# Fourteen quads of weight blocks by Strassen's seven products in a two-layer attention encoder

## The chip, the cores and the metric

The kernel runs on one core of one Trainium2 chip, as one launch. What counts is the device time of that core in microseconds. Below, TensorE is called PE, VectorE DVE, ScalarE ACT, SyncE SP and GpSimd POOL.

## The reference

x is 256 tokens by 4096 features, float32. There are two layers. In the first, h = rms_norm(x) is multiplied by w_in_ab (4096 x 13312) into queries, keys and values of two groups of attention heads (A: 16 query heads, 4 key heads, rotary positions; B: 16 heads in a neighbourhood with a bias) and a gate; y = attention x silu(gate), and x = x + y @ w_out_ab (4096 x 4096). The second is the same in form: w_in_c (4096 x 10240), 32 query heads and 8 key heads in a window with a sink, then x = x + y @ w_out_c. A last rms_norm is applied.

```
for layer in range(2):
    h = rms_norm(x, norm_w[layer])
    z = h @ w_in[layer]                       # q, k, v, gate
    y = attention(q, k, v) * silu(gate)       # (256, 4096)
    x = x + y @ w_out[layer]                  # (4096, 4096)
return rms_norm(x, final_norm_w)
```

## The kernel before, in words

Nearly all of the work is four matrix products of a 256 x 4096 activation with weights that are read once. Each operand is float32 and is cut into two parts of type fp32r, `hi` (rounded) and `lo` (the rest); a product takes three matmuls, hi x hi, hi x lo and lo x hi (`three_passes`, L1096, the matmuls on L1098, L1099 and L1100).

**Pairs and blocks.** `plan` (L155) cuts the columns into 31 pairs of two groups g = 0, 1 of 512 columns. A pair has NB = 32 blocks; a block (g, c) is the 256 rows 2c and 2c+1 (in chunks of 128) of one group, so 128 x 1024 elements in SBUF. `Pair.blocks` gives their order: `BLOCKS` (14 of group 0, 14 of group 1, then the last two of each) or `IN_TURN` (all 16 of group 0, then all of group 1). For a block PE does 2 row chunks x 2 token tiles x 3 passes = 12 matmuls of 512 columns into the two PSUM banks `proj[g][0]` and `proj[g][1]` (`product`, L1124). I number the pairs from 0; pair 6 is the first of `vg` columns, pairs 7 to 12 are a loop of three rounds of two pairs, 13 to 16 write x1 (14 to 16 a loop of three rounds), 17 to 26 are the second layer's input products, 27 to 30 write x2. The other loops hold one pair.

**How a block flows.** Every engine walks the same list of steps b = 0..31 of each pair, in program order. SP loads block b into ring slot b % 4 of `raw` once `w_lo` of block b-4 is made (`body`, L497). At step b, ACT makes `w_hi` of block b+2 when PE has done block b-2 (`split_hi_at`, L629, the activation on L637), then DVE makes `w_lo` of it (`split_lo`, L751, the subtraction on L757), and PE waits for `lo_ready`. When a group's last block is done, its two banks are drained: by ACT and, for v, DVE (`drain` L640, `drain_v` L785), or by DVE alone with the residual (`add_x1` L979, `add_x2` L1000). With `BLOCKS` group 0 is drained at step 30, with `IN_TURN` at step 16; group 1 at step 0 of the next pair.

**What else runs.** A pair with side A, B or C also holds the attention of four heads. One with side `qk`, `h` or `k` turns tiles: DVE transposes them at steps 0 and 3, they go through DRAM, and ACT and DVE split them at the third and fourth numbers of `BOTH_TURNS` or `K_TURN` (steps 5 and 9). The pairs with side "none" have only the drain. In the changed kernel no pair with attention has a quad.

The lines around the change:

```
if b == p.done0 and p.out == "x1":        # DVE, step b, after split_lo
    add_x1(0, p.n)
with eng.Fori(0, rounds) as i:            # a loop of the plan, on every engine
    for p in pairs:
        body(p.at(i))
```

## Time and profile before

| | us |
|---|---|
| median of 3 runs (lowest, highest) | 2814.05 (2813.85, 2814.28) |
| profiled execution, its own time | 2814.37 |
| its span, first to last instruction | 2812.6 |
| PE matmul busy | 2797.6 (99%), 12681 matmuls |
| DVE busy | 1687.7 (60%) |
| ACT busy | 1347.7 (48%) |
| DMA engines, mean share | 0.68 on the main queue, 226 GB/s of HBM |
| granted PE clock, mean | 0.998 |

The span leaves out 1.8 us that lie around the instructions. Matmuls overlap in the records: one is shown for 0.39 us though the next starts after 0.23 us, so the pace is read from start to start and not from the durations.

### The profile page before, as it was taken

What the parts mean: (1) busy time and instruction counts of PE and PEld (TensorE: products, weight loads), DVE (VectorE), ACT (ScalarE), POOL (GpSimd) and SP (SyncE); (2) the same over time, 40 slices, a digit from 0 to 9 for tenths busy, and PEclk for the clock granted to TensorE, in tenths of its full rate; (3) what the DMA queues carried; (4) which work ended last, traced back from release to release, by engine and by line L of the source; (5) the groups of instructions that cost most, each with busy time, mean ns of one, the idle gap of its engine ahead of it and who ended that gap; (6) DMA issues with size and microseconds to landing.
All of it is one profiled execution on the core that took longest, in us unless ns stands there. A gap on an engine that the chain in (4) does not pass through costs nothing.

```text
span 2812.6 us, 37759 instructions
## 1 busy us (share of the span) xinstructions
PE 2797.6 (99%) x12681; PEld 2329.4 (83%) x12681; DVE 1687.7 (60%) x2103; ACT 1347.7 (48%) x1654; POOL 16.4 (1%) x14
## 2 busy tenths in 40 slices
PE   9999999999999999999999999999999999999998
PEld 7888888888888888888888888888888888888886
DVE  7766666556556555566665556666655666665554
ACT  6455455445444444444443445555544455543333
POOL 0000000000000000000000000000000000000000
PEclk9999999999999999999999999999999999999999
DMA  9777777777767777677777767777676777676665
GB/s 334 222 210 232 225 226 221 224 217 228 234 209 215 228 220 239 189 254 254 253 240 222 223 211 218 231 233 220 221 226 204 231 227 225 216 251 218 215 209 187
DMA packets 357923, 637.17 MB, mean 227 GB/s; under 512 B 25376, under 2 KB 79136, under 8 KB 357792
## 3 DMA queue, kind: packets, MB, share of 16 engines
q1 hardware_dynamic: 343824, 593.52, 67.7%
q10 hardware_dynamic: 13968, 41.95, 4.1%
q8 instruction: 76, 1.25, 0.2%
q14 instruction: 55, 0.45, 0.1%
HBM read 585.56 MB, written 49.81 MB: 226 GB/s over the span
## 4 chain that ended last, share of the span: by engine, by line
PE 99%; DMA 0%; issue 0%; DVE 0%; ACT 0%; POOLq 0%; POOL 0%; SPq 0%; DVEq 0%; ACTq 0%
PE proj L1098 32%; PE proj L1099 32%; PE proj L1100 32%; PE o_ps L1099 1%; PE o_ps L1098 1%; PE sc_ps L1100 1%; PE o_ps L1100 1%; PE sc_ps L1099 1%; PE sc_ps L1098 1%; DMA raw<-in_w_in_ab 0%; DVE w_lo L757 0%; DVE x_fin L1091 0%; ACT w_hi L637 0%; POOLq L268 0%; POOL rms L598 0%
## 5 line engine op out<-in xcount | busy, mean ns | idle before, releaser
L757 DVE TENSOR_TENSOR w_lo<-raw,w_hi 128x1024 fp32r<-128x1024 f32 x990 | 1208.5, 1221 | 856.7 <-ACT w_hi L637 850.5
L637 ACT ACTIVATE w_hi<-raw 128x1024 fp32r<-128x1024 f32 x990 | 1049.6, 1060 | 1148.6 <-PE proj L1100 1087.3
L1098 PE MATMUL proj<-w_hi,h_hi 128*128 128x512 f32 x2936 | 1143.4, 389 | 2.0 <-issue 1.5
L1099 PE MATMUL proj<-w_lo,h_hi 128*128 128x512 f32 x2936 | 1142.8, 389 | 0.0
L1100 PE MATMUL proj<-w_hi,h_lo 128*128 128x512 f32 x2936 | 1142.1, 389 | 0.0
L1100 PEld LDWEIGHTS proj<-w_hi,h_lo 128*128 128x128 f32 x2936 | 551.2, 188 | 114.9
L1098 PEld LDWEIGHTS proj<-w_hi,h_hi 128*128 128x128 f32 x2936 | 551.4, 188 | 114.5 <-issue 2.4
L1099 PEld LDWEIGHTS proj<-w_lo,h_hi 128*128 128x128 f32 x2936 | 551.4, 188 | 109.9
L1098 PE MATMUL proj<-w_hi,y_hi 128*128 128x512 f32 x1024 | 398.4, 389 | 0.0
L1099 PE MATMUL proj<-w_lo,y_hi 128*128 128x512 f32 x1024 | 398.4, 389 | 0.0
L1100 PE MATMUL proj<-w_hi,y_lo 128*128 128x512 f32 x1024 | 398.3, 389 | 0.0
L1100 PEld LDWEIGHTS proj<-w_hi,y_lo 128*128 128x128 f32 x1024 | 192.2, 188 | 39.9
L1099 PEld LDWEIGHTS proj<-w_lo,y_hi 128*128 128x128 f32 x1024 | 192.3, 188 | 39.3
L1098 PEld LDWEIGHTS proj<-w_hi,y_hi 128*128 128x128 f32 x1024 | 192.3, 188 | 39.3
L912 DVE TENSOR_TENSOR y<-o_ps,head_land 128x256 f32<-128x256 f32 x64 | 27.2, 425 | 109.3 <-PE o_ps L1100 109.3
L736 ACT ACTIVATE y_hi<-y 128x256 f32 (+1 forms) x64 | 26.8, 419 | 94.9 <-DVE y L912 94.9
L704 ACT ACTIVATE probs<-sc_ps,exp_bias 128x256 f32<-128x256 f32 x96 | 44.7, 470 | 46.8 <-DVE exp_bias L899 34.7
L728 ACT ACTIVATE headT_hi<-head_land 128x512 fp32r<-128x512 f32 x64 | 40.5, 633 | 54.0 <-DMA head_land<-head_turn 51.6
L905 DVE TENSOR_TENSOR headT_lo<-head_land,headT_hi 128x512 fp32r<-128x512 f32 x64 | 43.9, 686 | 10.1 <-ACT headT_hi L728 9.8
L924 DVE STREAM_TRANSPOSE head_stage<-probs 128x512 f32<-128x512 f32 x64 | 44.3, 692 | 0.0
L887 DVE SCALAR_TENSOR_TENSOR sc_ps<-dist,slope,sc_ps 128x512 f32<-128x512 f32 x32 | 24.2, 756 | 28.9 <-PE sc_ps L1100 27.3
L891 DVE TENSOR_REDUCE neg_max<-sc_ps 128x2 f32<-128x512 f32 x48 | 33.2, 691 | 11.5 <-PE sc_ps L1100 9.6
(115 smaller groups left out, 975.5 us busy)
## 6 DMA issues: line engine op xcount, KB each, us to landing
raw<-in_w_in_ab SPq DMA_DIRECT2D x414, 512.0 KB, 4.4
raw<-in_w_in_c SPq DMA_DIRECT2D x320, 512.0 KB, 4.4
raw<-in_w_out_ab SPq DMA_DIRECT2D x128, 512.0 KB, 4.5
raw<-in_w_out_c SPq DMA_DIRECT2D x128, 512.0 KB, 4.5
head_turn<-head_stage SPq DMA_DIRECT2D x256, 96.0 KB, 1.9
head_land<-head_turn ACTq DMA_DIRECT2D x64, 384.0 KB, 5.5
landing<-group_turn ACTq DMA_DIRECT2D x31, 512.0 KB, 5.5
group_turn<-q_stage SPq DMA_DIRECT2D x64, 128.0 KB, 3.2
```

Source lines behind the costliest of these rows:

```text
L637: nc.scalar.activation(w_hi[:, slot], raw[:, slot], ACT.Copy).then_inc(hi_ready, 1)
L704: last = nc.scalar.activation(probs[:, t], sc_ps[:, t], ACT.Exp, bias=exp_bias[:, t:t + 1], scale=scale, accum_out=sums[:, t:t + 1])
L728: nc.scalar.activation(headT_hi[:, :, :2 * TT], head_land[:, :, :2 * TT], ACT.Copy) \
L736: nc.scalar.activation(y_hi[:, bass.ds(row, 1)].rearrange("p a n -> p (a n)"), y[:], ACT.Copy) \
L757: nc.vector.tensor_tensor(w_lo[:, slot], raw[:, slot], w_hi[:, slot].bitcast(F32), ALU.subtract) \
L891: nc.vector.tensor_reduce(dst[:], sc_ps[:], AX_X, ALU.max, negate=True).then_inc(maxima, 1)
L905: nc.vector.tensor_tensor(headT_lo[:, :, :2 * TT], head_land[:, :, :2 * TT], headT_hi[:, :, :2 * TT].bitcast(F32), ALU.subtract) \
L912: nc.vector.tensor_tensor(y[:].rearrange("p (t q r) -> p t q r", t=TT, q=NQ), o_ps[:].rearrange("p (t q r) -> p t q r", t=TT, q=NQ), gateT ...
L924: nc.vector.transpose(columns[:, :2 * TT], probs[:].rearrange("p t (k j r) -> p (t k) j r", k=TT, j=NQ))
L1098: nc.tensor.matmul(dst, hi, r_hi, start=start, stop=False)
L1099: nc.tensor.matmul(dst, hi, r_lo, start=False, stop=False)
L1100: return nc.tensor.matmul(dst, lo, r_hi, start=False, stop=stop)
```

## The change

Fourteen times four blocks, (0, c1), (1, c1), (1, c2), (0, c2), are taken together as a quad: a 2 x 2 arrangement of weight blocks B11, B12, B22, B21 and of activation tiles (two token tiles by two row pairs). Eight products of 6 matmuls become seven (the form of Winograd): four of the left factors are sums of activation tiles, made once for several pairs (`make_sums`, at the steps in `combine`), and the right factors are four blocks and three mixes of blocks, made by DVE in each quad. PE's product r reads slot (start + r/2) % 4 of `w_hi` and `w_lo` if r is even, else one of two spare slots (`weights_of`). SP, ACT, DVE and PE each keep four steps for a quad. PE's steps hold products 0 and 1, 2 and 3, 4 and 5, and 6. The products go to the banks x11, x12, x21, x22 (the old `proj`) and to three more, m1, m6, m7 (m7 shares the bank of `o_ps`).

After the last quad of a pair ACT copies m1 to SBUF and DVE folds m1, m6 and m7 into the four banks in seven additions (`fold`); the fifth completes x12. Group 1 starts after that, on the folded banks, at block `second_at`. I write q for the first block of a pair's last quad. Quads stand in pairs 6, 8 and 10 (`VG_QUADS`, q = 12, `second_at` = 18 = q+6), 14, 15, 16 and 28 (`X1_QUADS`, the same numbers), 18, 23 and 29 (`TWO_QUADS`, quads at 5 and 13, `second_at` = 20 = q+7) and 30 (`LAST_QUADS`, quad at 9, `second_at` = 16 = q+7). In these pairs group 0 is done and drained before group 1 begins, at step 18, 20 or 16. The counters `lo_ready`, `hi_ready` and `block_done` now count products, a quad for 8. The loop of two pairs has two rounds in place of three, its last two pairs stand alone, and so do the pairs of the loops of x1 and of x2. `K_TURN` splits at step 9 and not 5.

```diff
+def with_quads(first, second, end=()):
+    blocks, quads = [], {}
+    for e in first:
+        if isinstance(e, tuple):
+            c1, c2 = e
+            quads[len(blocks)] = e
+            blocks += [(0, c1), (1, c1), (1, c2), (0, c2)]
+        else:
+            blocks.append((0, e))
+    return blocks + [(1, c) for c in second] + list(end), quads
...
+REST1, REST2 = [0, 1, *range(4, KC // 2)], [0, 1, *range(6, KC // 2)]
+VG_QUADS = with_quads([*REST1[:12], (2, 3), *REST1[12:]], REST1)
+X1_QUADS = with_quads([*REST1[:12], (2, 3), *REST1[12:]], REST1)
+TWO_QUADS = with_quads([*REST2[:5], (2, 3), *REST2[5:9], (4, 5), *REST2[9:]], REST2)
+LAST_QUADS = with_quads([*REST1[:9], (2, 3), *REST1[9:-2]], REST1[:-2],
+                        [(g, EARLY + c) for g in range(2) for c in range(LATE)])
...
-K_NORM_TURN, K_TURN = (0, 5, 7, 10), (0, 0, 2, 5)
+K_NORM_TURN, K_TURN = (0, 5, 7, 10), (0, 0, 2, 9)
...
-        (1, [Pair("in_ab", vg(0), "vg", "qk", "qk", v=1)]),
-        (3, [Pair("in_ab", qk(1), "qk", "B", "vg", batch=4), Pair("in_ab", vg(1), "vg", "qk", "qk", v=2)]),
+        (1, [Pair("in_ab", vg(0), "vg", "qk", "qk", v=1, quads=VG_QUADS, heads=16, combine=((5, "vg", 0, 2),))]),
+        (2, [Pair("in_ab", qk(1), "qk", "B", "vg", batch=4),
+             Pair("in_ab", vg(1), "vg", "qk", "qk", v=2, quads=VG_QUADS, heads=20, heads_step=4)]),
+        (1, [Pair("in_ab", qk(3), "qk", "B", "vg", batch=6)]),
+        (1, [Pair("in_ab", vg(3), "vg", "qk", "qk", v=4)]),
         (1, [Pair("out_ab", out_cols(0), "x1", "B", "vg", batch=7)]),
-        (3, [Pair("out_ab", out_cols(1), "x1", "h", "x1", x_batch=0)]),
-        (1, [Pair("in_c", kvc(0), "kv", "h", "x1", x_batch=3)]),
-        (1, [Pair("in_c", c(0), "qg", "k", "kv", v=5)]),
+        (1, [Pair("out_ab", out_cols(1), "x1", "h", "x1", x_batch=0, quads=X1_QUADS, heads=32,
+                  combine=((6, "x1", 0, 2),))]),
+        (1, [Pair("out_ab", out_cols(2), "x1", "h", "x1", x_batch=1, quads=X1_QUADS, heads=32)]),
+        (1, [Pair("out_ab", out_cols(3), "x1", "h", "x1", x_batch=2, quads=X1_QUADS, heads=32, spare="x1_end")]),
+        (1, [Pair("in_c", kvc(0), "kv", "h", "x1", x_batch=3, combine=((15, "qg", 0, 2), (19, "qg", 1, 4)))]),
+        (1, [Pair("in_c", c(0), "qg", "k", "kv", v=5, quads=TWO_QUADS, heads=32)]),
         (3, [Pair("in_c", c(1), "qg", "C", "qg", batch=8)]),
         (1, [Pair("in_c", kvc(1), "kv", "C", "qg", batch=11)]),
-        (1, [Pair("in_c", c(4), "qg", "k", "kv", v=6)]),
+        (1, [Pair("in_c", c(4), "qg", "k", "kv", v=6, quads=TWO_QUADS, heads=48)]),
         (3, [Pair("in_c", c(5), "qg", "C", "qg", batch=12)]),
         (1, [Pair("out_c", out_cols(0), "x2", "C", "qg", batch=15)]),
-        (2, [Pair("out_c", out_cols(1), "x2", "none", "x2")]),
-        (1, [Pair("out_c", out_cols(3), "x2", "none", "x2")]),
+        (1, [Pair("out_c", out_cols(1), "x2", "none", "x2", quads=X1_QUADS, heads=64,
+                  combine=((6, "x2", 0, 2), (26, "x2", 1, 4)))]),
+        (1, [Pair("out_c", out_cols(2), "x2", "none", "x2", quads=TWO_QUADS, heads=64)]),
+        (1, [Pair("out_c", out_cols(3), "x2", "none", "x2", quads=LAST_QUADS, heads=64)]),
...
+def slot_free_after(p, m):
+    if m >= NB + RING:
+        return p.o + p.op[NB] + m - NB - RING + 1
+    return p.o + (p.ring_op[m - RING] if m >= RING else m - RING) + 1
...
+        def weights_of(p, start, r):
+            if r % 2 == 0:
+                slot = (start + r // 2) % RING
+                return w_hi[:, slot], w_lo[:, slot]
+            return [tile[:] for tile in spare_of[p.spare][r // 2 % 2]]
...
                 for b, (g, c) in enumerate(p.blocks):
-                    if isinstance(p.n, int) and p.n * NB + b < RING:
-                        pass
-                    else:
-                        sp.wait_ge(lo_ready, p.n * NB + b - RING + 1)
+                    if b >= RING and p.quad_at(b - RING) is not None and p.quad_at(b - RING)[2] < 3:
+                        k, _, part = p.quad_at(b - RING)
+                        sp.wait_ge(mixed, QUAD * (p.quad_n + k) + part + 1)
+                    elif b >= RING:
+                        sp.wait_ge(lo_ready, p.o + p.freed[b - RING])
+                    elif p.n0 > 0:
...
+            def quad_hi(p, k, start, part):
+                n = p.o + p.op[start]
+                (mix, mix3), mixes_done = mix_of[p.out], QUAD * (p.quad_n + k)
+                b11, _, b22, b21 = (raw[:, (start + r) % RING] for r in range(QUAD))
+                earlier = p.o + p.op[list(p.quads)[k - 1]] if k > 0 else None
+                def hi(r, source, count=1):
+                    if r % 2 == 0:
+                        act.wait_ge(block_done, slot_free_after(p, start + r // 2))
+                    elif r == 5:
+                        act.wait_ge(block_done, n + 2)
+                    elif earlier is not None:
+                        act.wait_ge(block_done, earlier + (6 if r == 1 else 4))
+                    elif r == 1:
+                        act.wait_ge(block_done, p.o)
+                        act.wait_ge(folded, p.folds)
+                        act.wait_ge(sums_split, p.combined + (1 if p.combine else 0))
+                    dst, _ = weights_of(p, start, r)
+                    nc.scalar.activation(dst, source, ACT.Copy).then_inc(hi_ready, count)
+                if part == 0:
+                    raw_landed(p, start)
+                    hi(0, b11)
+                if part == 1:
+                    raw_landed(p, start + 2)
+                    hi(1, b22)
+                if part == 2:
+                    act.wait_ge(mixed, mixes_done + 1)
+                    hi(2, mix[:])
+                    act.wait_ge(mixed, mixes_done + 2)
+                    hi(3, mix3[:])
+                if part == 3:
+                    raw_landed(p, start + 3)
+                    hi(4, b21)
+                    act.wait_ge(mixed, mixes_done + 3)
+                    hi(5, mix[:])
+                    act.wait_ge(mixed, mixes_done + 4)
+                    hi(6, b21, 2)
...
+            def copy_m1(p, b):
+                if p.quads and b == p.last_quad + QUAD:
+                    act.wait_ge(folded, p.folds)
+                    act.wait_ge(block_done, p.o + p.op[p.last_quad] + OPS)
+                    nc.scalar.activation(folds_of(p)[0], m1[:], ACT.Copy).then_inc(m1_copied, 1)
...
+            def quad_lo(p, k, start, part):
+                n = p.o + p.op[start]
+                mix, mix3 = (tile[:] for tile in mix_of[p.out])
+                mixes_done = QUAD * (p.quad_n + k)
+                b11, b12, b22, b21 = (raw[:, (start + r) % RING] for r in range(QUAD))
+                minus = lambda dst, a, b: nc.vector.tensor_tensor(dst, a, b, ALU.subtract)
+                def lo(r, source, count=1):
+                    hi, dst = weights_of(p, start, r)
+                    dve.wait_ge(hi_ready, n + r + 1)
+                    minus(dst, source, hi.bitcast(F32)).then_inc(lo_ready, count)
+                if part == 0:
+                    lo(0, b11)
+                if part == 1:
+                    second = (start + 1) % RING
+                    dve.wait_ge(raw_loaded[second], 16 * (p.n * (NB // RING) + (start + 1) // RING + (second > 1)))
+                    dve.wait_ge(lo_ready, n + 1)
+                    minus(mix, b12, b11).then_inc(mixed, 1)
+                    lo(1, b22)
+                if part == 2:
+                    dve.wait_ge(mixed, mixes_done + 1)
+                    minus(mix3, b22, b12).then_inc(mixed, 1)
+                    lo(2, mix)
+                    dve.wait_ge(mixed, mixes_done + 2)
+                    dve.wait_ge(lo_ready, n + 3)
+                    minus(mix, b22, mix).then_inc(mixed, 1)
+                    lo(3, mix3)
+                if part == 3:
+                    lo(4, b21)
+                    dve.wait_ge(mixed, mixes_done + 3)
+                    dve.wait_ge(lo_ready, n + 5)
+                    minus(b21, b21, mix).then_inc(mixed, 1)
+                    lo(5, mix)
+                    dve.wait_ge(mixed, mixes_done + 4)
+                    lo(6, b21, 2)
+                    dve.wait_ge(lo_ready, n + OPS)
...
+            def make_sums(p, b):
+                for k, (at, stage, quad, c1) in enumerate(p.combine):
+                    if b not in (at, at + 1):
+                        continue
...
+                    rows = slice(2 * c1, 2 * c1 + 4)
+                    a_hi, a_lo = (y_hi, y_lo) if p.w in ("out_ab", "out_c") else (h_hi, h_lo)
+                    dve.wait_ge(block_done, p.o)
+                    if p.out == "vg":
+                        dve.wait_ge(turned, p.x0 + 2)
+                    dve.wait_ge(sums_split, p.combined + k)
+                    nc.vector.tensor_tensor(parts, a_hi[:, rows].bitcast(F32), a_lo[:, rows].bitcast(F32), ALU.add) \
+                        .then_inc(sums_made, 1)
+                    a11, a12 = parts[:, 0:2, 0:P], parts[:, 2:4, 0:P]
+                    a21, a22 = parts[:, 0:2, P:SEQ], parts[:, 2:4, P:SEQ]
+                    s1, s2, s3, s4 = (sums[:, r] for r in range(4))
+                    dve.wait_ge(sums_made, done + 1)
+                    nc.vector.tensor_tensor(s3, a11, a21, ALU.subtract)
+                    nc.vector.tensor_tensor(s1, a21, a22, ALU.add).then_inc(sums_made, 1)
+                    dve.wait_ge(sums_made, done + 2)
+                    nc.vector.tensor_tensor(s2, s1, a11, ALU.subtract).then_inc(sums_made, 1)
+                    dve.wait_ge(sums_made, done + 3)
+                    nc.vector.tensor_tensor(s4, a12, s2, ALU.subtract).then_inc(sums_made, 1)
...
+            def fold(p, b):
+                add = lambda dst, a, b: nc.vector.tensor_tensor(dst, a, b, ALU.add).then_inc(folded, 1)
+                (x11, x21), (x12, x22) = [[bank[:] for bank in group] for group in proj]
+                f1, f2, f3 = folds_of(p)
+                if b == p.last_quad + QUAD:
+                    dve.wait_ge(m1_copied, p.pair_w + 1)
+                    dve.wait_ge(block_done, p.o + p.op[p.last_quad] + OPS)
+                    add(f2, m6[:], f1)
+                    dve.wait_ge(folded, p.folds + 1)
+                    add(f3, m7[:], f2)
+                if b == p.last_quad + QUAD + 1:
+                    dve.wait_ge(folded, p.folds + 2)
+                    add(f2, x22, f2)
+                    dve.wait_ge(folded, p.folds + 3)
+                    add(x22, x22, f3)
+                    add(x12, x12, f2)
+                if b == p.second_at:
+                    dve.wait_ge(block_done, p.o + p.op[p.second_at])
+                    add(x11, x11, f1)
+                    add(x21, x21, f3)
+                    dve.wait_ge(folded, p.folds + FOLDS)
...
+                if p.quads and b == p.second_at:
+                    pe.wait_ge(folded, p.folds + 5)
...
+            def quad(p, k, start, part):
...
+                def times(r, left, dst, first, final, count=1):
+                    right_hi, right_lo = weights_of(p, start, r)
+                    pe.wait_ge(lo_ready, n + r + 1)
+                    for j, (a_hi, a_lo) in enumerate(left):
+                        last = three_passes(dst[:], a_hi, a_lo, right_hi[:, j], right_lo[:, j],
+                                            first and j == 0, final and j == 1)
+                    last.then_inc(block_done, count)
+                if part == 0:
+                    if opens:
+                        pe.wait_ge(drained[1], 2 * p.n)
+                        pe.wait_ge(y_made, p.heads)
+                        pe.wait_ge(sums_split, p.combined + (1 if p.combine else 0))
+                    times(0, of_tile(c1, 0), m1, opens, closes)
+                    times(1, of_sum(3), x12, opens, closes)
+                if part == 1:
+                    times(2, of_sum(0), x22, opens, closes)
+                    times(3, of_sum(2), m7, opens, closes)
+                if part == 2:
+                    times(4, of_tile(c2, 0), x11, False, False)
+                    times(5, of_sum(1), m6, opens, closes)
+                if part == 3:
+                    times(6, of_tile(c2, 1), x21, False, False, 2)
...
```

## Rows read from the trace of the kernel before

**Rows 1.** The page: busy time of each engine, chain that ended last.
```profile
PE 2797.6 (99%) x12681; PEld 2329.4 (83%) x12681; DVE 1687.7 (60%) x2103; ACT 1347.7 (48%) x1654; POOL 16.4 (1%) x14
```

**Rows 2.** Waits of PE: line, releaser: us in total, times, longest.
```profile
PE proj L1098 <- issue: 1.5, 2, 0.8
PE proj L1098 <- DVE w_lo L757: 0.5, 1, 0.5
```

**Rows 3.** Timeline (start, us, instruction), PE, first matmuls of pairs 14 and 15.
```profile
1274.63 0.39 PE L1098 MATMUL proj<-w_hi,y_hi 128*128 128x512 f32 x1
...
1361.45 0.39 PE L1100 MATMUL proj<-w_hi,y_lo 128*128 128x512 f32 x1
1361.67 0.39 PE L1098 MATMUL proj<-w_hi,y_hi 128*128 128x512 f32 x1
```

**Rows 4.** Timeline, PE, at a back edge of the two-pair loop.
```profile
1000.50 0.39 PE L1100 MATMUL proj<-w_hi,h_lo 128*128 128x512 f32 x1
1001.64 0.49 PE L1098 MATMUL proj<-w_hi,h_hi 128*128 128x512 f32 x1 [0.76 <-issue]
1001.97 0.39 PE L1099 MATMUL proj<-w_lo,h_hi 128*128 128x512 f32 x1
```

**Rows 5.** Timeline of one block in pair 6: PE starts it; ACT; DVE.
```profile
588.10 0.39 PE L1098 MATMUL proj<-w_hi,h_hi 128*128 128x512 f32 x1
...
588.35 1.06 ACT L637 ACTIVATE w_hi<-raw 128x1024 fp32r<-128x1024 f32 x1 [1.66 <-PE proj L1100]
...
589.51 1.23 DVE L757 TENSOR_TENSOR w_lo<-raw,w_hi 128x1024 fp32r<-128x1024 f32 x1 [1.49 <-ACT w_hi L637]
```

**Rows 6.** Lines: instructions, count, busy us, mean ns, idle before.
```profile
L757 DVE TENSOR_TENSOR w_lo<-raw,w_hi 128x1024 fp32r<-128x1024 f32 x990 | 1208.5, 1221 | 856.7 <-ACT w_hi L637 850.5 <-DVE w_lo L757 1.0
...
L637 ACT ACTIVATE w_hi<-raw 128x1024 fp32r<-128x1024 f32 x990 | 1049.6, 1060 | 1148.6 <-PE proj L1100 1087.3 <-DMA raw<-in_w_in_ab 18.5 <-DMA head_turn<-head_stage 13.0
...
L887 DVE SCALAR_TENSOR_TENSOR sc_ps<-dist,slope,sc_ps 128x512 f32<-128x512 f32 x32 | 24.2, 756 | 28.9 <-PE sc_ps L1100 27.3 <-DVE w_lo L757 1.6
L651 ACT ACTIVATE za<-proj,rms 128x512 f32<-128x512 f32 x38 | 24.0, 684 | 31.5 <-PE proj L1100 31.5
...
L850 DVE TENSOR_TENSOR rope_swap<-za,table 128x256 f32<-128x256 f32 x20 | 7.2, 420 | 0.2
...
L985 DVE TENSOR_TENSOR za<-proj,za 128x512 f32<-128x512 f32 x8 | 5.2, 686 | 1.9 <-PE proj L1100 1.9
```

**Rows 7.** DMA issues: KB each, median us to landing.
```profile
raw<-in_w_out_ab SPq DMA_DIRECT2D x128, 512.0 KB, 4.5
```

**Rows 8.** Timeline, ACT, drain of a bank pair and the next w_hi.
```profile
553.00 1.27 ACT L651 ACTIVATE zb<-proj,rms 128x512 f32<-128x512 f32 x2 [1.67 <-PE proj L1100]
554.16 1.05 ACT L637 ACTIVATE w_hi<-raw 128x1024 fp32r<-128x1024 f32 x1
```

**Rows 9.** Timeline, DVE, adds after a w_lo; the residual drain of pair 28.
```profile
1362.17 1.29 DVE L985 TENSOR_TENSOR zb<-proj,zb 128x512 f32<-128x512 f32 x2 [0.25 <-DVE w_lo L757]
...
2629.57 1.29 DVE L1009 TENSOR_TENSOR za<-proj,x_fin 128x512 f32<-128x512 f32 x2 [0.36 <-DVE w_lo L757]
2630.89 0.69 DVE L1012 CUSTOM_DVE_ANT_0 swap<-za 128x512 f32<-128x512 f32 x1
...
2633.55 5.26 DVE L757 TENSOR_TENSOR w_lo<-raw,w_hi 128x1024 fp32r<-128x1024 f32 x4
```

**Rows 10.** Timeline near 17 us: DVE releases a waiting PE.
```profile
16.50 2.59 DVE L757 TENSOR_TENSOR w_lo<-raw,w_hi 128x1024 fp32r<-128x1024 f32 x2 [0.53 <-ACT w_hi L637]
...
17.78 0.50 PE L1098 MATMUL proj<-w_hi,h_hi 128*128 128x512 f32 x1 [0.49 <-DVE w_lo L757]
```

**Rows 11.** Timeline, pair 14: DVE's w_lo of blocks 11 to 13; PE starts block 12.
```profile
1300.47 3.93 DVE L757 TENSOR_TENSOR w_lo<-raw,w_hi 128x1024 fp32r<-128x1024 f32 x3
...
1307.28 0.39 PE L1098 MATMUL proj<-w_hi,y_hi 128*128 128x512 f32 x1
```

**Rows 12.** Timeline, PE: the nine warm-up matmuls at the start.
```profile
1.46 3.93 PE L1104 MATMUL proj<-spin 128*128 128x512 f32 x9 [1.46 <-DVE spin L792]
```

More of the change, by code:

```diff
@@ L119, with __init__ @@
 class Pair:
-    def __init__(self, w, cols, out, side, before, batch=None, x_batch=None, v=None):
+    def __init__(self, w, cols, out, side, before, batch=None, x_batch=None, v=None, quads=None,
+                 heads=0, heads_step=0, combine=(), spare=None):
         self.w, self.cols, self.out, self.side, self.before = w, cols, out, side, before
@@ L138, in __init__, with quad_at @@
         self.blocks = IN_TURN if out in ("qg", "vg") else STARTING if before is None else BLOCKS
+        self.quads, self.combine, self.spare = {}, combine, spare or out
+        if quads is not None:
+            self.blocks, self.quads = quads
         self.done0 = self.blocks.index((0, KC // 2 - 1)) + 1
+        self.heads0, self.heads_step = heads, heads_step
+        self.op, self.ring_op, self.freed, op = [], [], [], 0
+        for b in range(NB):
+            start = next((q for q in self.quads if q <= b < q + QUAD), None)
+            self.op.append(op)
+            self.ring_op.append(op if start is None else op + 2 * (b - start))
+            if start is None:
+                self.freed.append(op + 1)
+                op += 1
+            else:
+                self.freed.append(op + OPS)
+                op += OPS if b == start + QUAD - 1 else 0
+        self.op.append(op)
+        self.second_at = None
+        if self.quads:
+            self.last_quad = max(self.quads)
+            self.second_at = next(b for b in range(self.last_quad + QUAD, NB) if self.blocks[b][0] == 1)
+    def quad_at(self, b):
+        for k, q in enumerate(self.quads):
+            if q <= b < q + QUAD:
+                return k, q, b - q
+        return None
     def at(self, i):
@@ L193, in plan @@
         n += rounds * len(pairs)
+        ops += rounds * pairs[0].o_step
+        quads += rounds * pairs[0].quad_step
+        folds += rounds * pairs[0].folds_step
         x += rounds * x_step
@@ L643, in drain @@
+            def drain(p, g, out):
+                act.wait_ge(block_done, p.o + p.op[p.done0] if g == 0 else p.o)
+                if g == 0 and p.quads:
+                    act.wait_ge(folded, p.folds + FOLDS)
                 for t in range(TT):
@@ L686, in body @@
                             act.wait_ge(summed, 4 * 4 + 1)
-                        drain(p, 0, p.out, p.n)
+                        drain(p, 0, p.out)
                     for m, k in turns_at(p, b, 2):
@@ L1034, in body @@
                         first_x(p.blocks[b + AHEAD][1])
+                    make_sums(p, b)
                     split_lo(p, b)
+                    if p.quads:
+                        fold(p, b)
                     if p.n0 == 0:
@@ L1144, in product @@
                     last = three_passes(proj[g][t][:], hi[:, k, toks], lo[:, k, toks], w_hi[:, slot, j],
-                                        w_lo[:, slot, j], k == 0, k == KC - 1)
+                                        w_lo[:, slot, j], k == 0 and not (p.quads and g == 1),
+                                        k == KC - 1 or b + 1 == p.second_at and j == 1, bool(p.quads) and g == 1)
                 last.then_inc(block_done, 1)
+            def quad(p, k, start, part):
+                n = p.o + p.op[start]
+                c1, c2 = p.quads[start]
+                hi, lo = (y_hi, y_lo) if p.w in ("out_ab", "out_c") else (h_hi, h_lo)
+                s_hi, s_lo = sums_of[p.out][k]
+                (x11, x21), (x12, x22) = proj
+                opens, closes = k == 0, start == p.last_quad
+                of_tile = lambda c, t: [[tile[:, 2 * c + j, t * P:(t + 1) * P] for tile in (hi, lo)] for j in range(2)]
+                of_sum = lambda r: [[tile[:, r, j] for tile in (s_hi, s_lo)] for j in range(2)]
+                def times(r, left, dst, first, final, count=1):
[20 more added lines that the diff above has]
+                    times(6, of_tile(c2, 1), x21, False, False, 2)
@@ L1206, in body @@
                             last_blocks(p)
+                    elif p.quad_at(b) is not None:
+                        quad(p, *p.quad_at(b))
                     else:
```

172 lines of the change are left out of this document (131 added, 41 removed).

## The prediction

> **What bounds the kernel now.** I read the page's busy times first: PE is busy for 2797.6 of 2812.6 us, DVE and ACT for 60% and 48% [rows 1]. Then the waits of PE, to see whether that share hides pauses: there are almost none, 1.5 us for "issue" in two places and 0.5 us for a `w_lo` [rows 2]. So the number of matmuls times their pace is the time. The timeline gives the pace: pair 14 runs from 1274.63 to 1361.67, 87.04 us for 384 matmuls, so 0.2267 us for one and 2.72 us for a block of 12 [rows 3]. A change can gain only by fewer matmuls, and whatever makes PE wait is paid in full.
>
> How far ahead the others are decides what they can take on. In a steady block PE starts at 588.10, ACT begins the next free `w_hi` 0.25 us later, and DVE the `w_lo` at 589.51, done at 590.7 [rows 5]. That block is used three blocks after 588.10, at 596.26: a lead of 5.5 us. DVE spends 1.22 us of each 2.72, so a backlog shrinks by 2.72 - 1.35 = 1.37 us a block; 1.35 is the pitch of four `w_lo` in a backlog, (5.26 - 1.22)/3 [rows 9].
>
> **Matmuls removed.** 14 quads x (48 - 42) = 84 matmuls x 0.2267 = -19.0 us [rows 3]. A product is 6 matmuls, 1.36 us; a quad takes 9.52 us in place of 10.88.
>
> **A back edge removed.** PE's two "issue" waits [rows 2] are the two back edges of the two-pair loop: 1001.64 - 1000.50 is 1.14 us where 0.23 is the pace, and the matmul behind it takes 0.33, 0.10 over the pace [rows 4], 1.0 us in all. Two rounds have one back edge, so -1.0; between 0 and -2.0, since the bodies change. The x1 loop's back edge shows nothing: 1361.45 to 1361.67 is the ordinary pace [rows 3], so unrolling it and the x2 loop gives 0. The Trainium skill (Runtime: NRT & Kernel Launch, "Instruction fetch mechanics") says that a taken branch to a target outside the fetch window stalls the engine. By that alone the three back edges of the one-pair loops would be gains too, 3.0 us more; the row disagrees for these, and agrees for the two-pair loop.
>
> **Inside a quad.** ACT makes 7 `w_hi`, DVE 11 subtractions of 1024 elements (7 `w_lo`, 4 mixes), where there were 4 and 4. I count from the start of product 0. `w_lo` 0 is done at -5.6, the steady lead. An operation that waits for the one before costs 1.22 + 0.13; one that doesn't starts 0.08 before the other's end, as two adds of 0.69 take 1.29 [rows 9]. That gives: first mix -4.3, `w_lo` 1 -3.1, second mix -2.0, `w_lo` 2 -0.9, third mix 0.5, `w_lo` 3 1.6, `w_lo` 4 2.8, fourth mix 4.1. Product 5 uses product 1's spare slot, so its `w_hi` starts 0.25 behind that one's end at 2.72, is done at 4.0, and its `w_lo` at 5.3. The last is done at 6.5, those of blocks q+4 and q+5 at 7.8 and 9.15. PE wants them at 1.36r: product 3 at 4.1, 5 at 6.8, 6 at 8.2, block q+4 at 9.5. The least margin is 1.5 us. B22 and B21 must have landed: their loads start at the `w_lo` of q-2 and q-1, -11.0 and -8.3, and take 4.5 us [rows 7]; wanted at -6.9 and -1, so only the first is late, by 0.4, which the mix before it hides. Cost 0 with this cover; a DVE 1.5 us later than steady would show.
>
> It is later in one place. In pair 14 the `w_lo` of block 12, second of three that end at 1304.40, is done at 1303.05, 4.2 us ahead of 1307.28 [rows 11]: 1.4 late at the start of the quad. `make_sums` at step 6 (one add of 1.22 and four of 0.42 [rows 6], then 1.22 for the low part) takes 4.2 us more there and pushes the second split of the turned tile by 0.4. So `w_lo` 5 comes at 7.0 for 6.8: +0.4 with PE's restart (below; 0 to 1.5). The other sums fall where DVE has its full lead or regains it by step 12: 0.
>
> **The folds, the large term.** Time is now from E, when the quad's last matmul is issued out and block q+4 starts. Group 1 waits for the fifth addition. The order is fixed by ACT's and DVE's queues: ACT's copy of m1 stands ahead of the `w_hi` of q+6, and DVE's first addition stands behind the `w_lo` of q+6, which waits for that `w_hi`.
> - ACT starts the copy at 0.25 [rows 5], the `w_hi` 0.58 later (two drains of 0.68 took 1.16 to the next start [rows 8]), done at 0.83 + 1.06 = 1.89.
> - DVE starts the `w_lo` of q+6 0.10 later [rows 5]: 1.99 to 3.21.
> - Two additions (m6, m7): a gap of 0.25 behind three waits as at 1362.17, 0.69 each as L985 [rows 6, 9], 0.03 between dependent ones (2630.86 to 2630.89 [rows 9]): done at 4.87.
> - Step q+5: the `w_lo` of q+7 comes ahead of the rest, to 6.00.
> - Three additions: gap 0.13, to 6.82, to 7.54, and the third, independent, to 8.14.
> - PE starts 0.06 later (16.50 + 1.22 to 17.78 [rows 10]), at 8.20, and its first matmul costs 0.10 more.
>
> With `second_at` = q+6 PE wants to start at 2 x 2.72 = 5.44. It waits 8.20 - 5.44 + 0.10 = 2.86 us, in seven pairs (6, 8, 10, 14, 15, 16, 28): +20.0. Behind the wait stand all matmuls; nothing overlaps them. With q+7 (pairs 18, 23, 29, 30) it wants 8.16: 0.14 each, +0.6. Bounds: with DVE's shortest gaps 2.65, times seven 18.6; an addition that writes PSUM isn't in the trace except as L887, 0.76 [rows 6], and with that for all five and gaps of 0.36 [rows 9] it is 3.5, times seven 24.5, and 0.7 x 4 = 2.8 for the others. I take the nearest rows, L985's. A gain is excluded, since both queues are in order.
>
> **The drains that move.** Group 0's drain now comes at `second_at`, behind two more additions (1.29). For x2 it is `add_x2`, 3.98 us to the next `w_lo` (2629.57 to 2633.55), behind a gap of 0.36 [rows 9]. In pair 29: `w_lo` q+8 at 9.27, q+9 at 10.62, additions to 12.04, drain from 12.40, `w_lo` of q+10 at 16.38 + 1.22 = 17.6, wanted at 6 x 2.72 = 16.32. +1.4 with the restart (0 to 2.5). In pair 28 the same comes at 16.25 for 16.46, as PE has already lost 2.86. Next pairs profit in lead, not in time. For x1, v and q the drain is 1.3 to 2.6 us, covered by at least 0.8: 0. SP's residual and final loads (steps 14 and 19) land before the earlier drains; the split moved to step 9 is covered as those of `qk` are: 0.
>
> **Sum.** -19.0 - 1.0 + 20.0 + 0.6 + 0.4 + 1.4 = +2.4. On the profiled execution's own 2814.37 (span 2812.6 and 1.8 around it) that is 2816.8; the median shown is 0.3 lower, so I say 2816.4. A difference under 0.2%, 5.6 us, can't be told from none.
>
> **Rivals.**
> - *The stall halts the clock (slower).* Place: the seven waits of 2.9 us. For it: PE has no pause that long in this trace, so nothing shows that the clock stays up. Against: behind the 1.1 us at the back edge the next pitch is 0.33 and then ordinary [rows 4]. If after each wait PE ran as in its warm-up, nine matmuls in 3.93 us against 2.04 at pace [rows 12], it is 1.9 us x 7 = +13: 2830. It decides if the 2.4 GHz level doesn't outlast the wait. The Trainium skill (TensorE: Matmul & The Clock Gate, "Part 1: The HAM clock gate") says that an idle array goes back to 1.2 GHz; by it this cost would come with long enough waits, which no row here shows. Chance 0.10.
> - *The quads starve (slower).* If the six dependent operations of a quad have gaps of 0.36 and not 0.13 and B22 lands a microsecond later, the 1.5 us of margin are gone and each quad stalls some 0.8: +11, 2827. For: the mixes wait for two semaphores each. Against: the leads of 5.5 us. Chance 0.12.
> - *The fold is in time (faster).* If the order of the queues is not what holds it, PE loses nothing at `second_at`, and only the other terms stay: -20.0 + 1.8, 2796; half of it 2806. For: DVE is idle for 2.4 us before its `w_lo` of q+6. Against: the copy must come after E, and behind it alone 1.06 + 5 x 0.69 + 2 x 1.22 = 6.95 us stand for 5.44. Chance 0.12.
> - The forecast: 0.66, of which 0.02 lie under -0.2%, 0.10 over +0.2% by the upper bounds (2821), 0.54 between.
>
> Faster 0.02 + 0.12 = 0.14; within 0.54; slower 0.10 + 0.10 + 0.12 = 0.32. The forecast's own range is 2813 to 2822; with the rivals up to the point where 2 in 10 are left out, 2806 to 2826.
>
> **What would show it.** PE matmuls 12597. In the waits of PE, seven of about 2.7 us for a DVE addition in `fold`, the rest small, 20 us in all; right if the first group-1 matmul stands 8.2 us behind E. One "issue" wait. Wrong: waits for `w_lo` inside the quads of 0.5 us or more (starved), a pitch of 0.43 behind the folds (clock), or a PE total of waits under 12 us (fold in time). If an addition on two banks takes over 0.8 us, the term is 24 and the kernel slower.

## The result and the profile after

The changed kernel takes 2824.44 us (median of 8 runs, 2821.31 to 2827.58) against 2814.10 (8 runs, 2813.85 to 2814.79): a ratio of 1.0037, with a 95% interval of 1.0026 to 1.0048. It is slower by 10 us. One run of the experiments (E3, 3079.68 us at a granted clock of 0.85) is left out of its comparison. I had said 2816.4 with a range of 2806 to 2826 and "no change" as the likeliest: the time lies near the upper end of the range, and the side, slower by over 0.2%, had 0.32.

The profiled execution took 2825.39 us, its span is 2823.6. The busy times answer to [rows 1], the waits of PE to [rows 2]:

```profile
PE 2788.7 (99%) x12597; PEld 2316.4 (82%) x12597; DVE 1873.5 (66%) x2314; ACT 1399.2 (50%) x1713; POOL 17.2 (1%) x14
```
```profile
PE proj L1412 <- DVE proj L1051: 16.8, 7, 2.7
PE m L1412 <- DVE spare_c_lo L984: 1.7, 3, 0.6
...
PE o_bank L1412 <- DVE spare_c_lo L984: 1.2, 2, 0.7
PE o_bank L1412 <- DVE spare_x_lo L984: 0.8, 1, 0.8
PE m L1412 <- DVE spare_x_lo L984: 0.8, 2, 0.6
PE proj L1412 <- DVE w_lo L984: 0.6, 1, 0.6
PE proj L1412 <- DVE spare_x_lo L984: 0.3, 1, 0.3
PE proj L1412 <- DVE w_lo L974: 0.3, 1, 0.3
```

The 84 matmuls are gone. The first row of waits is the fold (L1051 is its addition, L984 the subtraction of a quad), seven times; the others are products inside quads that wait for their `w_lo`, a kind that I had forecast at one place only, and in the last row the block behind the drain of pair 29. No "issue" row is left. A row of waits counts from the end of the matmul before, so the loss is more than it shows: I sum the distances from start to start beyond 0.227 us (columns: what, and us against the kernel before).

| | us against the kernel before |
|---|---|
| 84 matmuls | -19.1 |
| back edges, two of 1.0 | -2.0 |
| seven waits for the fold (six of 2.50, 2.86 in pair 28), and 0.1 at each restart | +18.5 |
| waits for `w_lo` in the quads of pairs 18, 23 and 29, with restarts | +8.8 |
| the earlier drain of pair 29, with restart | +0.6 |
| matmuls at 0.427 us, 22 in three groups, with their edges | +4.8 |
| start of the program, smaller things | -0.6 |
| sum (span: 2823.6 - 2812.6) | +11.0 |

The fold in pair 14. E is 1319.31; PE restarts at 1327.26. These are the timelines (start, duration) of ACT, DVE and PE:

```profile
1319.59 0.60 ACT L838 ACTIVATE parts_v<-m 128x512 f32<-128x512 f32 x1 [1.29 <-PE proj L1414]
1320.09 1.05 ACT L789 ACTIVATE w_hi<-raw 128x1024 fp32r<-128x1024 f32 x1
```
```profile
1321.24 1.23 DVE L974 TENSOR_TENSOR w_lo<-raw,w_hi 128x1024 fp32r<-128x1024 f32 x1 [1.11 <-ACT w_hi L789]
1322.51 0.69 DVE L1051 TENSOR_TENSOR parts_v<-m,parts_v 128x512 f32<-128x512 f32 x1
1323.23 0.69 DVE L1051 TENSOR_TENSOR sums_v<-o_bank,parts_v 128x512 f32<-128x512 f32 x1
1323.84 1.22 DVE L974 TENSOR_TENSOR w_lo<-raw,w_hi 128x1024 fp32r<-128x1024 f32 x1
1325.09 0.69 DVE L1051 TENSOR_TENSOR parts_v<-proj,parts_v 128x512 f32<-128x512 f32 x1
1325.82 0.70 DVE L1051 TENSOR_TENSOR proj<-proj,sums_v 128x512 f32<-128x512 f32 x1
1326.42 0.69 DVE L1051 TENSOR_TENSOR proj<-proj,parts_v 128x512 f32<-128x512 f32 x1
```
```profile
1324.53 0.39 PE L1414 MATMUL proj<-w_hi,y_lo 128*128 128x512 f32 x1
1327.26 0.47 PE L1412 MATMUL proj<-w_hi,y_hi 128*128 128x512 f32 x1 [2.34 <-DVE proj L1051]
```

This is the chain of the prediction, in its order: the copy ahead of the `w_hi`, the `w_lo` ahead of the first addition, another `w_lo` between the second and the third. It ends 7.8 us behind E where I had 8.14, and the wait is 2.73 - 0.23 = 2.50 us. In six of the seven pairs PE restarts at E + 7.94, in pair 28 at E + 8.30.

Behind three of the seven waits PE then ran slowly. The timeline of pair 6, and two windows of 8 us around the folds of pairs 6 and 8 (columns: window, length, busy us of PE, PEld, DVE, ACT, POOL, granted clock, DMA share, GB/s):

```profile
602.02 0.47 PE L1412 MATMUL proj<-w_hi,h_hi 128*128 128x512 f32 x1 [2.34 <-DVE proj L1051]
...
602.80 0.63 PE L1412 MATMUL proj<-w_hi,h_hi 128*128 128x512 f32 x1
603.23 0.63 PE L1413 MATMUL proj<-w_lo,h_hi 128*128 128x512 f32 x1
...
605.79 0.57 PE L1413 MATMUL proj<-w_lo,h_hi 128*128 128x512 f32 x1
606.20 0.39 PE L1414 MATMUL proj<-w_hi,h_lo 128*128 128x512 f32 x1
606.43 0.39 PE L1412 MATMUL proj<-w_hi,h_hi 128*128 128x512 f32 x1
```
```profile
599.00:607.00 8.00, 5.66 (x19) 4.25 (x18) 6.95 (x10) 2.65 (x5) 0.00 (x0) 0.79 0.61 189
782.00:790.00 8.00, 5.66 (x26) 4.33 (x25) 6.94 (x10) 2.65 (x4) 0.00 (x0) 1.00 0.57 179
```

From 602.80 to 605.79 the matmuls start 0.43 us apart, and the granted clock of that window is 0.79 for 1.00 in the other: part of it was at the 1.2 GHz level, the lower of the two. 26 matmuls fit into the second window and 19 into the first. Each group of seven or eight costs 1.6 us.

### The profile page after: what moved, and what is told of

The parts are those of the page before. It is cut to its first block, busy times and chain, and to the rows that moved or that the text cites. A ratio compares the mean times of both kernels' runs of the same rounds, so it can differ in the third digit from the quotient of the medians.

```text
span 2823.6 us, 36505 instructions
## 1 busy us (share of the span) xinstructions
PE 2788.7 (99%) x12597; PEld 2316.4 (82%) x12597; DVE 1873.5 (66%) x2314; ACT 1399.2 (50%) x1713; POOL 17.2 (1%) x14
## 4 chain that ended last, share of the span: by engine, by line
PE 92%; DVE 5%; DMA 2%; ACT 1%; issue 1%; DVEq 0%; POOLq 0%; POOL 0%; ACTq 0%; SPq 0%
PE proj L1412 29%; PE proj L1413 29%; PE proj L1414 29%; DVE w_lo L974 1%; DMA raw<-in_w_in_c 1%; PE o_bank L1413 1%; PE o_bank L1412 1%; PE o_bank L1414 1%; DVE w_lo L984 1%; PE sc_ps L1414 1%; PE sc_ps L1413 1%; PE sc_ps L1412 1%; DMA raw<-in_w_out_c 0%; ACT w_hi L789 0%; DVE spare_c_lo L984 0%
## 5 line engine op out<-in xcount | busy, mean ns | idle before, releaser
L974 DVE TENSOR_TENSOR w_lo<-raw,w_hi 128x1024 fp32r<-128x1024 f32 x934 | 1139.7, 1220 | 658.2 <-ACT w_hi L789 651.1
L789 ACT ACTIVATE w_hi<-raw 128x1024 fp32r<-128x1024 f32 x934 | 989.8, 1060 | 946.6 <-PE proj L1414 866.7
L1412 PE MATMUL proj<-w_hi,h_hi 128*128 128x512 f32 x2852 | 1113.0, 390 | 7.2 <-DVE proj L1051 7.0
L1413 PE MATMUL proj<-w_lo,h_hi 128*128 128x512 f32 x2852 | 1112.3, 390 | 0.0
L1414 PE MATMUL proj<-w_hi,h_lo 128*128 128x512 f32 x2852 | 1111.5, 390 | 0.0
L1412 PEld LDWEIGHTS proj<-w_hi,h_hi 128*128 128x128 f32 x2852 | 536.2, 188 | 117.0 <-DVE proj L1051 5.5
L1412 PE MATMUL proj<-w_hi,y_hi 128*128 128x512 f32 x940 | 368.1, 392 | 10.0 <-DVE proj L1051 9.7
L1413 PE MATMUL proj<-w_lo,y_hi 128*128 128x512 f32 x940 | 367.5, 391 | 0.0
L1414 PE MATMUL proj<-w_hi,y_lo 128*128 128x512 f32 x940 | 367.3, 391 | 0.0
L1223 DVE TENSOR_TENSOR y<-o_bank,head_land 128x256 f32<-128x256 f32 x64 | 27.2, 424 | 113.3 <-PE o_bank L1414 113.3
L812 ACT ACTIVATE w_hi<-raw 128x1024 fp32r<-128x1024 f32 x42 | 44.3, 1055 | 39.8 <-DVE raw L984 20.0
L984 DVE TENSOR_TENSOR w_lo<-raw,w_hi 128x1024 fp32r<-128x1024 f32 x42 | 51.4, 1223 | 15.8 <-ACT w_hi L812 13.9
```

The lines of the kernel that those rows point to most:

```text
L789: nc.scalar.activation(w_hi[:, slot], raw[:, m % RING], ACT.Copy).then_inc(hi_ready, 1)
L812: nc.scalar.activation(dst, source, ACT.Copy).then_inc(hi_ready, count)
L974: nc.vector.tensor_tensor(w_lo[:, slot], raw[:, m % RING], w_hi[:, slot].bitcast(F32), ALU.subtract) \
L984: minus = lambda dst, a, b: nc.vector.tensor_tensor(dst, a, b, ALU.subtract)
L1223: nc.vector.tensor_tensor(y[:].rearrange("p (t q r) -> p t q r", t=TT, q=NQ), o_ps.rearrange("p (t q r) -> p t q r", t=TT, q=NQ), gateT, A ...
L1412: nc.tensor.matmul(dst, hi, r_hi, start=start, stop=False, skip_group_check=more)
```

## The experiments

E0 and E1 test whether the slow groups are the clock's answer to the idle array; E2 and E3 what makes the wait; E4 whether the pairs with two quads starve with one; E5 and E6 put it together; E8 the back edge. E1, E2, E4 and E8 ran on one chip, on which the kernel before took 2814.45 us (31 runs, 2812.84 to 2817.01); E0, E3, E5 and E6 on another, with 2814.15 (11 runs, 2813.09 to 2815.76).

### E1: PE kept at work during the wait

```diff
+FILL = 11
...
                 if p.quads and b == p.second_at:
+                    if p.second_at == p.last_quad + 6:
+                        for _ in range(FILL):
+                            nc.tensor.matmul(sc_ps[:].rearrange("p t n -> p (t n)"), hi[:, 0, 0:P], w_hi[:, slot, 0],
+                                             start=True, stop=True)
                     pe.wait_ge(folded, p.folds + 5)
```

> The changed kernel with 11 matmuls of 512 columns (2.5 us at the full pace) put into sc_ps, which no one reads, ahead of PE's wait for the fifth addition in the seven pairs where group 1 starts at q+6. In the profiled run of the changed kernel that wait is 2.6 us seven times, and behind three of them (603, 1504, 2599 us) PE runs 7 or 8 matmuls at 427 ns instead of 227, 1.6 us each. Theory: the idle array sometimes loses its 2.4 GHz level, and this makes both the time above my sum and the spread of 2821 to 2828. Then with PE kept at work the additions end as before, no matmul runs at 427 ns, and the time is 2825.4 - 3 x 1.65 = 2820.4, all runs within 1 us. Rival: the slow stretches come from the additions on the banks or from the restart itself: they stay, the median stays at 2824 and so does the spread.

2821.31 us (10 runs, 2819.04 to 2822.28), ratio 1.0023 (1.0014 to 1.0033). The timeline of its PE in pair 6, where E is 594.58, and the window of 8 us around this fold:

```profile
599.79 0.39 PE L1415 MATMUL proj<-w_hi,h_lo 128*128 128x512 f32 x1
600.02 2.66 PE L1448 MATMUL sc_ps<-w_hi,h_hi 128*128 128x512 f32 x11
602.51 0.42 PE L1413 MATMUL proj<-w_hi,h_hi 128*128 128x512 f32 x1
602.77 0.39 PE L1414 MATMUL proj<-w_lo,h_hi 128*128 128x512 f32 x1
603.00 0.39 PE L1415 MATMUL proj<-w_hi,h_lo 128*128 128x512 f32 x1
```
```profile
599.00:607.00 8.00, 8.00 (x37) 6.50 (x36) 6.99 (x10) 3.06 (x4) 0.00 (x0) 1.00 0.64 215
```

Group 1 starts at E + 7.93, no earlier than before, and the clock of the window is 1.00. There is no slow group behind any fold. The mean granted clock of the whole run is 0.999 in nine of the ten runs and 0.998 in one; in the eight runs of the changed kernel it is 0.996 to 0.998. So the slow groups come from the idle array. The time is 0.9 us above what I had said. One back edge shows its 1.1 us again here, which would explain that much; the waits in the quads moved too, as they do from profile to profile (6.0 us here for 8.8). The spread is 3.2 us for 6.3; I had said 1, but the kernel before spread by 4.2 on this chip.

### E0: the changed kernel again

> The changed kernel as it stands, on the chip of the other three runs of this group, for a comparison on one chip. Theory (an idle array sometimes loses its 2.4 GHz level): seven waits of 2.5 us again at the same places, and behind some of them, not the same ones as in the first profile, 7 to 9 matmuls at 427 ns; median 2824, single runs between 2820 (no such stretch) and 2832 (all seven). Rival (the slow stretches belong to the places): behind the same three waits, at 602, 1504 and 2598 us.

2826.38 us (5 runs, 2822.41 to 2828.56), ratio 1.0039 (1.0026 to 1.0051). Seven waits at the same places, six of 2.50 us and 2.85 in pair 28. The slow groups stood behind the folds of pairs 6, 16 and 28, the same three as in the first profile, as the rival had it and against my theory that they change from run to run; in E4, which has the same code up to pair 16, it was 6, 15 and 28. E1 shows that the idle is needed; the four folds without a slow group show that it isn't enough. What chooses among them stays open, and so does what moves single runs between 2821 and 2829 us.

### E2: ACT's copy behind the next w_hi

```diff
-                    copy_m1(p, b)
                     ...
                     split_hi_at(p, b)
+                    copy_m1(p, b)
```

> The changed kernel with ACT's copy of m1 behind the w_hi of block q+6 and not ahead of it; nothing else. Theory: the wait at second_at is made by the order on ACT (copy, then w_hi, then DVE's w_lo of q+6, and only then the first addition). With the w_hi made ahead of the quad's end, the first addition starts at E + 0.9 and not E + 3.2; the chain is 0.9 + 1.4 + 1.2 + 2.0 + 0.15 = 5.7 for 5.44, so the wait falls from 2.6 to 0.3 us in seven pairs, -16, and the 427 ns stretches go with it: 2820.4 - 16 = 2804, below the kernel before by 10 us. Rival: DVE's seven operations themselves are the chain and the copy is hidden among them: under 1 us of each wait goes, 2817 or more, with the slow stretches still there.

2806.71 us (10 runs, 2806.08 to 2809.86), ratio 0.9973 (0.9964 to 0.9983): 18 us off the changed kernel, and below the kernel before; I had said 2804. DVE and PE in pair 14, where E is 1312.20:

```profile
1312.29 1.22 DVE L974 TENSOR_TENSOR w_lo<-raw,w_hi 128x1024 fp32r<-128x1024 f32 x1
1313.55 0.69 DVE L1051 TENSOR_TENSOR parts_v<-m,parts_v 128x512 f32<-128x512 f32 x1
1314.28 0.69 DVE L1051 TENSOR_TENSOR sums_v<-o_bank,parts_v 128x512 f32<-128x512 f32 x1
1314.88 1.22 DVE L974 TENSOR_TENSOR w_lo<-raw,w_hi 128x1024 fp32r<-128x1024 f32 x1
...
1317.47 0.69 DVE L1051 TENSOR_TENSOR proj<-proj,parts_v 128x512 f32<-128x512 f32 x1
```
```profile
1317.41 0.39 PE L1414 MATMUL proj<-w_hi,y_lo 128*128 128x512 f32 x1
1318.30 0.47 PE L1412 MATMUL proj<-w_hi,y_hi 128*128 128x512 f32 x1 [0.50 <-DVE proj L1051]
```

The `w_lo` ahead of the first addition starts at once and not at E + 1.9, and the fifth addition ends 6.0 us behind E. The wait is 0.66 us here and 0.3 to 1.5 in the seven pairs, more than my 0.3, because DVE still has a backlog from the quad (the `w_lo` of q+6 starts at E + 0.1 and not before). No slow group is left: waits of up to 1.5 us cost no clock.

### E3: the last additions ahead of the w_lo of q+7

```diff
+                    if p.quads and b == p.last_quad + QUAD + 1:
+                        fold(p, b)
                     split_lo(p, b)
-                    if p.quads:
+                    if p.quads and b != p.last_quad + QUAD + 1:
                         fold(p, b)
```

> As the run with ACT's copy behind the w_hi of q+6, and DVE's third to fifth addition ahead of the w_lo of q+7 in step q+5. In that run's trace the seven waits at second_at are still 0.4 to 1.6 us with the restart, 5.7 us in all; it gave 2806.7 us. Theory: what is left of the wait is this w_lo (1.2 us) between the additions; without it the fifth addition ends 4.5 us behind E for 5.44, no wait is left, and the time is 2806.7 - 5.7 = 2801. Rival: the w_lo of q+7, now 2 us later, is missed by PE at q+7 or the loads tied to it come late: then waits for w_lo take the place of those for the addition and the time stays above 2804.

2802.61 us (five runs compared, 2800.86 to 2803.08), ratio 0.9956 (0.9943 to 0.9969). Its PE still waits 0.4 us for the fold in pair 6 and 0.3 in pair 14, and 0.5 for a `w_lo` behind the drain in pair 28: 1.2 us and 0.3 for the restarts, 1.5 of the 1.6 us that are missing from my 2801. The `w_lo` of q+7, the rival's, is waited for nowhere.

### E4: one quad in pairs 18, 23 and 29

```diff
-TWO_QUADS = with_quads([*REST2[:5], (2, 3), *REST2[5:9], (4, 5), *REST2[9:]], REST2)
+TWO_QUADS = with_quads([*REST1[:11], (2, 3), *REST1[11:]], REST1)
```

> The changed kernel with one quad at block 11 in place of two at 5 and 13 in pairs 18, 23 and 29 (11 quads in all, second_at = 18 = q+7). In the changed kernel PE waits for w_lo inside the quads of these three pairs: 2.1, 2.7 and 3.9 us in start-to-start times, 0.6 more in pair 29 behind its drain, 9.3 in all. Theory: the second quad comes four blocks behind the first, before DVE has regained its lead, and the loads, which wait for w_lo, are late with it. With one quad the 9.3 us go and 18 matmuls (4.1 us) come back: 2824.4 - 5.2 = 2819.2, with waits for w_lo under 1 us in all. Rival: a single quad starves as well (DVE's 13 us for 9.5 of PE), then some 1 us stays in each and the time is 2822; or the lateness has nothing to do with the number of quads, then it is 2828.

2821.36 us (11 runs, 2817.92 to 2822.59), ratio 1.0022 (1.0013 to 1.0031). The waits of its PE:

```profile
PE proj L1412 <- DVE proj L1051: 16.4, 7, 2.3
...
PE proj L1412 <- DVE w_lo L974: 0.6, 2, 0.3
PE m L1412 <- DVE spare_x_lo L984: 0.2, 1, 0.2
```

In pairs 18, 23 and 29 the waits in the quads are gone. The 0.2 us that is left (0.5 from start to start, with the restart) lies in the one quad of pair 28, and in E0 the one quad of pair 14 lost as much: a single quad can starve a little too. The ratio fell from 1.0037 and 1.0039 in the two series of the changed kernel to 1.0022, 4.5 us for my 5.2, though the intervals overlap; 0.6 of my 9.3 us, the drain of pair 29 with its restart, is still there. The edit changes two things, the number of quads and the place of the first, block 11 for block 5. One quad alone at block 5 wasn't tried.

### E5 and E6: both reorderings, with one quad, and with two quads five blocks apart

> Both reorderings, and one quad at block 11 in place of two in pairs 18, 23 and 29. Theory: starting from the 2801 expected with the reorderings alone, the 8.5 us that PE waits for w_lo in the quads of these pairs go, and 4.1 us of matmuls come back: 2796.6, 11 quads. Rival: the two kinds of wait share a cause, and with the fold out of the way the two quads starve less: then the gain is small or none, 2801 or more.

2798.22 us (5 runs, 2796.71 to 2799.11), ratio 0.9942 (0.9929 to 0.9955). This is the fastest, 16 us below the kernel before, with 11 quads for 14. I had said 2796.6; E3 was 1.6 above its figure already, and the step from E3 to E5 is 4.4 us, as forecast. The rival, that the quads would starve less with the fold out of the way, is false. The waits of its PE beside the one at the start of the program:

```profile
PE proj L1414 <- DVE w_lo L974: 0.8, 2, 0.4
PE proj L1414 <- DVE proj L1051: 0.3, 1, 0.3
```

The edit of E6 beside those of E3:

```diff
+TWO_QUADS = with_quads([*REST2[:5], (2, 3), *REST2[5:10], (4, 5), *REST2[10:]], REST2)
```

> Both reorderings, and the second quad of pairs 18, 23 and 29 one block later (blocks 5 and 14, five blocks between them; second_at = q+6). Theory (DVE has not regained its lead): it regains 1.37 us a block, so of the 6.5 us that the three second quads cost, some 1.4 us each go, 4 in all: 2797; the first quads' waits stay. Rival: the second quad is late because its loads are, which wait for w_lo of four blocks before; then one block more does not help, 2801.

2801.40 us (5 runs, 2799.60 to 2802.19), ratio 0.9954 (0.9941 to 0.9967): 1.2 us better than E3 with the quads four blocks apart, while I had said 4, and 3 worse than one quad. The intervals of E3 and E6 overlap, so the profiles have to tell more than the medians. In its profile the second quads cost 0.7 us in pair 18, none in 23 and 1.2 in 29, with restarts, where in E3 it was 1.0, 0.7 and 3.2: 3.0 us less, so that part of the theory holds. Against it stand 1.1 us of new waits for the fold, which group 1 now wants at q+6 in these pairs too, and 0.7 behind the drain of pair 29. The first quads still starve, with 1.0, 0.8 and 0.4 us.

### E8: the kernel before with the new loops

```diff
-        (3, [Pair("in_ab", qk(1), ...), Pair("in_ab", vg(1), ...)]),
+        (2, [Pair("in_ab", qk(1), ...), Pair("in_ab", vg(1), ...)]),
+        (1, [Pair("in_ab", qk(3), "qk", "B", "vg", batch=6)]),
+        (1, [Pair("in_ab", vg(3), "vg", "qk", "qk", v=4)]),
```

and the x1 and x2 loops written out (arguments are left out in these lines).

> The kernel before, without any quad, with the loops of the changed one: two rounds of the two-pair loop and its last two pairs alone, the x1 and x2 loops unrolled. The changed kernel's trace shows no issue wait at any back edge, where I had predicted one of 1.0 us. Theory: the gap at the back edge depends on where the loop's code lies, and it vanishes here too or stays once: 2812.1 (both gone) or 2813.1 (one stays). Rival: unrolling costs instruction fetch elsewhere, then 2814 or more.

2813.01 us (11 runs, 2811.35 to 2814.41), ratio 0.9994 (0.9985 to 1.0003), 1.4 us less, which alone isn't clear of noise. PE at the one back edge:

```profile
819.50 0.39 PE L1105 MATMUL proj<-w_hi,h_lo 128*128 128x512 f32 x1
820.82 0.49 PE L1103 MATMUL proj<-w_hi,h_hi 128*128 128x512 f32 x1 [0.93 <-issue]
```

The profile has one gap, of 1.1 us, where the kernel before has two of 0.9. The gap stays here and in E1; it isn't there in the changed kernel and the other runs of it, whose loops have the same two pairs. So my term of -1.0 is right for the round that is gone. The second microsecond comes and goes from build to build; what in the code decides it wasn't tried.

## Why the prediction was right and wrong

- **Matmuls removed, -19.0.** Right: 12597 matmuls at the same pace.
- **Back edge, -1.0.** -2.0, within my bound.
- **The folds, +20.0.** Right in mechanism and place; 18.5 measured. That is the lower bound of 18.6 that I gave. The gap of 0.25 before the first addition was 0.04 in pair 14 (0.19 in pairs 8 and 10), and the copy took 0.60 and not 0.68, with the `w_hi` 0.50 behind its start for my 0.58. PE's answer took 0.15 for my 0.06 (0.05 in pairs 8 and 10). E2 and E3 show the cause: ACT's order was worth 18 us, 5 of them by the clock, DVE's 4 to 5.
- **q+7 pairs, +0.6.** None: the wait at `second_at` stands seven times and not eleven.
- **The drain of pair 29, +1.4.** 0.6.
- **Inside a quad, 0, and pair 14, +0.4.** Here the prediction failed for pairs 18, 23 and 29 (8.8 us), while pair 14 lost nothing in the first profile and 0.5 us in E0. The step is "B22 and B21 must have landed ... only the first is late, by 0.4". Counted from product 0, ACT could start on B22 at -6.0 only in pairs 8, 10 and 30, and at -4.2 to -4.8 in the other pairs with one quad, which was still enough. In the six quads that starved it was -3.7 and later (columns: when B22's load was issued and how long it took to land, when ACT started on B22, all from product 0, and what PE lost):

  | quad | issued | landing | ACT starts | lost |
  |---|---|---|---|---|
  | pair 18, first | -9.8 | 6.1 | -3.7 | 0.3 |
  | pair 18, second | -7.5 | 5.3 | -2.2 | 1.8 |
  | pair 23, first | -9.8 | 6.6 | -3.2 | 0.8 |
  | pair 23, second | -7.5 | 5.1 | -2.4 | 1.9 |
  | pair 29, first | -8.2 | 4.6 | -3.6 | 0.5 |
  | pair 29, second | -8.6 | 8.1 | -0.5 | 3.4 |

  I had the load issued at -11.0 and landed in 4.5 [rows 7]. Both were off: the load went out 1.2 to 3.5 us late and, in five of six, took 0.6 to 3.6 longer. In pair 18 the `w_lo` that frees the slot stands behind the turned tile's transpose and the drain at the head of the pair:

```profile
1631.71 1.41 DVE L1100 SCALAR_TENSOR_TENSOR v_lo<-proj,rms,v_hi 128x512 fp32r<-128x512 f32 x2 [0.28 <-ACT v_hi L858]
1633.17 1.23 DVE L974 TENSOR_TENSOR w_lo<-raw,w_hi 128x1024 fp32r<-128x1024 f32 x1
```

  The load is issued at 1634.42. The chain then reads:

```profile
1640.55 1.06 ACT L812 ACTIVATE spare_c_hi<-raw 128x1024 fp32r<-128x1024 f32 x1 [3.13 <-DMA raw<-in_w_in_c]
```
```profile
1641.64 1.22 DVE L984 TENSOR_TENSOR spare_c_lo<-raw,spare_c_hi 128x1024 fp32r<-128x1024 f32 x1 [1.56 <-ACT spare_c_hi L812]
...
1648.84 1.23 DVE L984 TENSOR_TENSOR raw<-raw,mix_q 128x1024 f32<-128x1024 f32 x1
1649.98 1.22 DVE L984 TENSOR_TENSOR spare_c_lo<-mix_q,spare_c_hi 128x1024 fp32r<-128x1024 f32 x1
```

  DVE stands idle for 1.56 us until B22 is there, and the `w_lo` of product 5 ends at 1651.20, that is 6.9 behind product 0 at 1644.26, for 6.8. The second quad comes while the first one's backlog is still there, and its loads wait for the late `w_lo`s. I had used the landing's median where a quad needs four landings in a row, and the steady lead at block 5, where it isn't there yet: in the six profiles with a quad there ACT starts at -4.4 to -2.2, 17 times of 18 later than -4.0, while at block 11 of the same pairs (E4, E5) it starts at -6.3 or earlier. So both count, the place at the head of a pair (1.6 of the 8.8 us, the first quads) and the quad just before (7.2, the second ones). The rest of the step was right. By my chain ACT starts on B22 at -5.5 with 1.5 us to spare, so PE should begin to lose time at -4.0. In all 106 quads of the eight profiles of kernels with quads, a start of -4.2 or earlier cost PE nothing, and a later one cost 4.0 us less the lead, within 0.2; the second quad of pair 23 lost up to 0.4 more.
- **The rival of the clock, 0.10.** It came true in part: 1.6 us a time, near my 1.9, but three times and not seven. I had treated it as all or nothing.
- **The rival of the starving quads, 0.12.** True in three pairs, with 8.8 us near its 11, and by its second condition (B22 late), not by its first: the gaps between dependent operations were 0.10 to 0.14. B22 was late by 1.8 us and more and not by one, and the stalls were six of 0.3 to 3.4 us and not fourteen of 0.8, so that the sum comes near 11 is luck.
- **The fold in time, 0.12.** False; E3 shows what it takes.

On the profiled execution I was 8.6 us short (2816.8 for 2825.4). Two rivals that each came true in part give 4.8 and 8.8 us; the folds, the q+7 pairs, the drain, pair 14 and the back edge were 1.5, 0.6, 0.8, 0.4 and 1.0 better, which leaves 9.3, and the start of the program took 0.6 off. That the time still lies in my range is in part luck: neither loss is in the sum, the upper end was there for the rivals' sake, and terms that came out smaller hid a third of them.
